# A decoder kernel's last feed-forward product turned to tokens by features, with the final norm done per token block

## The chip, the cores and the metric

The kernel runs on one core of a Trainium2 chip. The metric is the device time of one execution in microseconds; the kernel before takes 2560.55 us in the median of 3 runs (2559.9 to 2560.63). Everything is computed in float32 accuracy: each matrix product is made of three products of a high part and a low part (hi x hi, hi x lo, lo x hi), which TensorE takes in its fp32r form.

## What is computed

The reference is a decoder trunk for 1024 tokens of 1024 features: one recurrent layer, one attention layer, a SwiGLU feed-forward behind each, and a final RMSNorm. Cut to what the change touches (layer 1's feed-forward and the norm):

```python
def rmsnorm(x, g):
    y = x * lax.rsqrt(jnp.mean(x * x, axis=-1, keepdims=True) + EPS)
    return y * g

def swiglu(x, w_in, w_out):
    gate, up = jnp.split(x @ w_in, 2, axis=-1)
    return (jax.nn.silu(gate) * up) @ w_out

    # h: (1, 1024 tokens, 1024 features)
    h = h + mix
    h = h + swiglu(rmsnorm(h, norm_ffn[1]), w_ffn_in[1], w_ffn_out[1])   # D_FF = 2816
    return rmsnorm(h, norm_final)
```

## The kernel before

The residual `resid` lies in SBUF with features on the partitions: `resid[:, k, :]` holds features 128k to 128k+127 of all 1024 tokens. All products are made in that layout: weights are the stationary operand, 128 features by 128, and the tokens are the moving one, 512 at a time. A PSUM tile `ps[0]` to `ps[3]` is 128 x 1024 float32 (two banks), and a table of turns, `tiles`, says which of the four each step uses; `claim` (line 610) makes TensorE wait until the tile's last reader has counted up `drained`. Weight pieces go through four slots `raw`, `wh`, `wl` in the same way: SyncE loads them (`load`, line 427), ScalarE makes the high half (`split_hi`, line 963, its copy is line 974), VectorE the low half (`split_lo`, line 1316).

The feed-forward of layer 1 is `ffn(1)`, written for each engine. It runs over 11 groups of 256 hidden features. In each group from the second on, TensorE makes the gate tile G0, the eight output tiles of the group before (from `hh` and `hl`, the halves of the hidden values), the up tile U0, and then G1 and U1. An input tile (`in_tile`) is 48 matmuls of 128x512, an output tile 12. VectorE scales the gate (line 1353), ScalarE takes silu (1128), VectorE scales the up tile, multiplies (1581), ScalarE makes `hh` (1132), VectorE `hl` (1585); and VectorE adds each output tile to the residual (`add_tile`, line 1359). On ScalarE and VectorE the last group is written out behind the loop; on TensorE it is in the loop.

Behind the last group stands `out_epilogue` (line 693): the last group's own output tiles, 8 tiles of 12 matmuls. The first parts of three tiles, which need only the first half of the hidden values, are made ahead of the wait for the second half. Beside it the final norm is made ready. ScalarE squares each finished residual tile (line 994), GpSimd adds pairs of squares (line 578), and TensorE sums over features by 80 matmuls of one column against ones (`stat`, line 663), queued among the output tiles. VectorE multiplies the residual tiles by the final gain (`final_gain`, line 1547). Then a root (line 999) and a reciprocal (line 1346) give the factor of each token, TensorE transposes the residual, eight transposes of 128x128 for each of 8 token blocks (line 957), ScalarE and VectorE read one half of each block out of PSUM with the factor (lines 1304 and 1793), and SyncE stores it (line 510), 512 KB at a time, out of four buffers `tmp`.

The order on each engine is the order in which the program is written; there is no scheduler. The lines that matter for the turns are these:

```python
tiles.plan(f"ffn{f}A", [0, 1, 2, 3]).plan(f"ffn{f}L", [0, 1, 2, 3] * 3, GROUPS - 1, 1)
tiles.plan(f"ffn{f}E", OUT_STAT)        # OUT_STAT = [0, 1, 2, 0, 1, 2, 0, 1, 3]
tiles.plan("final", [0, 1, 2, 3] * 2)
```

Of the kernel before, what the change touches and what calls it, by code (L numbers as in the profile page):

```python
# [4 lines left out]
F32 = mybir.dt.float32  # L5
# [71 lines left out]
def hawk_fox_yoco(nc, x, norm_mix, norm_ffn, w_ffn_in, w_ffn_out, w_rec_in, conv_w, conv_b,  # L77
# [26 lines left out]
    V_MIX, V_FFN, V_KV, V_FINAL = 0, 2 * KT, 4 * KT, 5 * KT  # L104
    V_CONVB, V_LRU, V_CONVW, V_GATEB = 6 * KT, 7 * KT, 8 * KT, (8 + TAPS) * KT
# [27 lines left out]
    tiles.plan("final", [0, 1, 2, 3] * 2)  # L133
# [4 lines left out]
    STAT = {"start": 0, "recE": 1, "ffn0E": 2, "attE": 3, "ffn1E": 4}  # L138
# [6 lines left out]
    with ExitStack() as life:  # L145
# [9 lines left out]
        with ExitStack() as early:  # L155
            lru_alt = [sb(f"lru_alt{k}", [P, S], F32, early) for k in range(4)]
# [11 lines left out]
        row_rstd = sb("row_rstd", [P, QB], F32)  # L168
# [39 lines left out]
        hl = sb("hl", [P, 2, S], F32R)  # L208

# [81 lines left out]
        gained = sem("gained")  # L291
        rows_filled = sem("rows_filled")
        rows_ready = [sem(f"rows_ready{j}") for j in range(2)]
        rows_stored = [sem(f"rows_stored{b}") for b in range(4)]
# [37 lines left out]
        LRU_LAST = [tmp, lru_alt]  # L332
# [45 lines left out]
        def mean_of(seg):  # L378

            if seg == "ffn1E":  # L380
                return row_rstd[:, :], ps[3][:, 0:QB]
# [44 lines left out]
        def _(sp):  # L426
# [80 lines left out]
            for b in range(QB):  # L507
                for j in range(2):
                    sp.wait_ge(rows_ready[j], b + 1)
                sp.dma_start(out[0, b * P:(b + 1) * P, :], tmp[b % 4][:, :]).then_inc(rows_stored[b % 4], 16)  # L510
            for b in range(4):
                sp.wait_ge(rows_stored[b], 16 * (QB // 4))
# [3 lines left out]
        def _(pool):  # L516
# [86 lines left out]
            sum_squares("ffn1E")  # L603
# [3 lines left out]
        def _(pe):  # L607
# [43 lines left out]
            def stat(seg, n):  # L651
# [8 lines left out]
                if seg == "ffn1E":  # L660
# [1155 lines left out]
```

## Time and profile before

| what | value |
|---|---|
| median of 3 runs | 2560.55 us (2559.9 to 2560.63) |
| the profiled execution, its own time | 2558.25 us |
| its span, first to last instruction | 2556.4 us |
| TensorE matmul busy | 2446.8 us, 96% of the span |
| VectorE busy | 1271.8 us, 50% |
| ScalarE busy | 786.1 us, 31% |
| GpSimd busy | 124.8 us, 5% |
| mean granted TensorE clock | 0.98 of full |
| bytes moved | 122.63 MB, 48 GB/s on average |

In the page, PE is TensorE's matmuls, PEld its weight loads, DVE VectorE, ACT ScalarE, POOL GpSimd and SP SyncE. Times of rows are microseconds from the span's start. Where a row merges instructions, "x12" is how many; a matmul's duration is longer than the distance to the next one, since they are pipelined. A bracket at the end of a row is the idle time of the engine before it, and whom it waited for. A granted clock of 1.00 is 2.4 GHz, 0.50 is 1.2 GHz.

### The profile page before, as it was taken

What the parts mean: (1) busy time and instruction counts of PE and PEld (TensorE: products, weight loads), DVE (VectorE), ACT (ScalarE), POOL (GpSimd) and SP (SyncE); (2) the same over time, 40 slices, a digit from 0 to 9 for tenths busy, and PEclk for the clock granted to TensorE, in tenths of its full rate; (3) what the DMA queues carried; (4) which work ended last, traced back from release to release, by engine and by line L of the source; (5) the groups of instructions that cost most, each with busy time, mean ns of one, the idle gap of its engine ahead of it and who ended that gap; (6) DMA issues with size and microseconds to landing.
All of it is one profiled execution on the core that took longest, in us unless ns stands there. A gap on an engine that the chain in (4) does not pass through costs nothing.

```text
span 2556.4 us, 28698 instructions
## 1 busy us (share of the span) xinstructions
PE 2446.8 (96%) x11353; PEld 2009.7 (79%) x11353; DVE 1271.8 (50%) x1257; ACT 786.1 (31%) x1045; POOL 124.8 (5%) x80
## 2 busy tenths in 40 slices
PE   7999889999999999998999999979999999999998
PEld 5788768888888888867777777767788888888887
DVE  5767674434333434466665656553434444444344
ACT  4543542111111111145555555542211111111112
POOL 1000010000000000011110111001000000000001
PEclk9999999999999999999999999979999999999999
DMA  3111011111111111120111101021211111111111
GB/s 116 58 58 49 25 33 50 49 49 46 44 49 49 49 49 49 34 83 25 34 34 34 33 26 32 25 85 55 58 50 49 49 43 47 49 49 49 49 33 66
DMA packets 167166, 122.63 MB, mean 48 GB/s; under 512 B 5072, under 2 KB 148672, under 8 KB 167104
## 3 DMA queue, kind: packets, MB, share of 16 engines
q1 hardware_dynamic: 165360, 117.52, 15.1%
q10 hardware_dynamic: 1744, 4.32, 0.6%
q8 instruction: 35, 0.57, 0.1%
q14 instruction: 27, 0.22, 0.0%
HBM read 113.37 MB, written 8.45 MB: 48 GB/s over the span
## 4 chain that ended last, share of the span: by engine, by line
PE 88%; DVE 5%; ACT 3%; issue 3%; ACTq 1%; DMA 0%; POOL 0%; DVEq 0%
PE ps L619 66%; PE ps L804 8%; PE ps L915 3%; PE ps L851 3%; PE ps L838 2%; PE ps L819 1%; PE ps L667 1%; PE ps L816 1%; ACT kh L1190 1%; DVE rstd L1346 1%; DVE kv_tmp L1716 0%; PE ps L663 0%; DVE wl L1316 0%; DVE resid L1359 0%; ACT kh L1195 0%
## 5 line engine op out<-in xcount | busy, mean ns | idle before, releaser
L619 PE MATMUL ps<-xh,wh 128*128 128x512 f32 x1680 | 523.5, 393 | 10.6 <-DVE wl L1316 10.1
L619 PE MATMUL ps<-xl,wh 128*128 128x512 f32 x1680 | 518.2, 390 | 0.0
L619 PE MATMUL ps<-xh,wl 128*128 128x512 f32 x1680 | 518.0, 389 | 0.0
L619 PEld LDWEIGHTS ps<-xh,wh 128*128 128x128 f32 x1680 | 315.1, 188 | 81.4 <-issue 16.4
L1353 DVE TENSOR_TENSOR tmp<-ps,rstd 128x1024 f32<-128x1024 f32 x96 | 117.3, 1224 | 506.0 <-PE ps L619 506.0
L619 PEld LDWEIGHTS ps<-xh,wl 128*128 128x128 f32 x1680 | 315.7, 188 | 65.9
L619 PEld LDWEIGHTS ps<-xl,wh 128*128 128x128 f32 x1680 | 315.7, 188 | 65.7
L1359 DVE TENSOR_TENSOR resid<-ps,resid 128x1024 f32<-128x1024 f32 x216 | 261.6, 1222 | 187.9 <-PE ps L619 187.5
L974 ACT ACTIVATE wh<-raw 128x1024 fp32r<-128x1024 f32 x193 | 201.6, 1049 | 402.2 <-PE ps L619 349.7
L1316 DVE TENSOR_TENSOR wl<-raw,wh 128x1024 fp32r<-128x1024 f32 x193 | 238.8, 1241 | 169.6 <-ACT wh L974 169.5
L619 PE MATMUL ps<-hh,wh 128*128 128x512 f32 x704 | 219.4, 393 | 1.7 <-DVE hl L1585 1.7
L619 PE MATMUL ps<-hl,wh 128*128 128x512 f32 x704 | 217.8, 391 | 0.0
L619 PE MATMUL ps<-hh,wl 128*128 128x512 f32 x704 | 217.7, 390 | 0.0
L1132 ACT ACTIVATE hh<-tmp 128x1024 fp32r<-128x1024 f32 x44 | 46.7, 1061 | 480.1 <-DVE tmp L1581 480.1
L804 PE MATMUL ps<-xh,wh 128*128 128x512 f32 x384 | 160.1, 417 | 8.7 <-DVE wl L1316 5.5
L619 PEld LDWEIGHTS ps<-hh,wh 128*128 128x128 f32 x704 | 132.6, 189 | 31.2 <-DVE hl L1585 2.5
L619 PEld LDWEIGHTS ps<-hh,wl 128*128 128x128 f32 x704 | 132.8, 189 | 27.8
L619 PEld LDWEIGHTS ps<-hl,wh 128*128 128x128 f32 x704 | 132.7, 189 | 27.8
L804 PE MATMUL ps<-xh,wl 128*128 128x512 f32 x384 | 153.1, 399 | 0.0
L804 PE MATMUL ps<-xl,wh 128*128 128x512 f32 x384 | 153.0, 398 | 0.0
L1128 ACT ACTIVATE tmp<-tmp 128x1024 f32<-128x1024 f32 x44 | 46.6, 1059 | 322.9 <-DVE tmp L1353 322.9
L1734 DVE TENSOR_TENSOR ptl<-ps,pth 128x512 fp32r<-128x512 f32 (+1 forms) x160 | 98.3, 635 | 76.3 <-ACT pth L1253 74.8
(186 smaller groups left out, 2792.2 us busy)
## 6 DMA issues: line engine op xcount, KB each, us to landing
raw<-in_w_ffn_in SPq DMA_DIRECT2D x88, 512.0 KB, 3.8
raw<-in_w_ffn_out SPq DMA_DIRECT2D x44, 512.0 KB, 3.3
raw<-in_w_rec_in SPq DMA_DIRECT2D x16, 512.0 KB, 4.0
raw<-in_w_kvf SPq DMA_DIRECT2D x16, 512.0 KB, 3.9
xin<-in_x SPq DMA_DIRECT2D x4, 1024.0 KB, 10.1
raw<-in_w_rec_out SPq DMA_DIRECT2D x8, 512.0 KB, 4.0
raw<-in_w_q SPq DMA_DIRECT2D x8, 512.0 KB, 3.7
spill<-resid SPq DMA_DIRECT2D x8, 512.0 KB, 2.6
```

Source lines behind the costliest of these rows:

```text
L619: last = pe.matmul(acc[:, h], w, v[:, h], start=(first and p == 0), stop=(final and p == 2))
L804: last = pe.matmul(acc, w, v[:, k, h], start=(k == 0 and p == 0), stop=(k == KT - 1 and p == 2))
L838: last = pe.transpose(t_ps[t % 2][:, col + (q - q0) * P:col + (q - q0 + 1) * P], probs[u % 2][:, q, kb * P:(kb + 1) * P], ident[:, :])
L851: last = pe.matmul(o_ps[:, q0 * P:2 * P], v, pt[t % 2][:, col:col + n], start=(kb == 0 and pt is pth), stop=(kb == 2 * r + 1 and pt is ptl))
L915: last = pe.matmul(acc[:, h], w, ohl[:, k, v, h], start=(k == 0 and p == 0), stop=(k == KT - 1 and p == 2))
L974: act.activation(wh[slot][:, :], raw[slot][:, :], ACT.Copy).then_inc(hi_ready[slot], 1)
L1128: act.activation(tmp[t][:, :], tmp[t][:, :], ACT.Silu).then_inc(silu_ready, 1)
L1132: act.activation(hh[:, t, :], tmp[2 + t][:, :], ACT.Copy).then_inc(hh_ready, 1)
L1316: dve.tensor_tensor(wl[slot][:, :], raw[slot][:, :], wh[slot][:, :].bitcast(F32), ALU.subtract).then_inc(lo_ready[slot], 1)
L1353: dve.tensor_tensor(dst, ps[slot][:, :], rstd[:, :], ALU.mult).then_inc(drained[slot], 1)
L1359: dve.tensor_tensor(resid[:, m, :], ps[slot][:, :], resid[:, m, :], ALU.add).then_inc(drained[slot], 1)
L1734: dve.tensor_tensor(ptl[t % 2][:, 0:width], t_ps[t % 2][:, 0:width], pth[t % 2][:, 0:width].bitcast(F32), ALU.subtract).then_inc(ptl_ready, 1)
```

## The change

The last group's product is made the other way round. In `token_epilogue` a block of 128 tokens of `hh` or `hl` is the stationary operand, and the rows of the output weights (512 features at a time) are the moving one, so that a PSUM tile holds 128 tokens by 1024 features. That needs the residual in the same layout, and so it is transposed ahead: on TensorE the last group is written out behind the loop with tile turns of its own (`ffn1Z`), and `turn_block` puts four blocks of eight transposes behind its U0 tile and four behind its G1 tile. ScalarE copies each transposed block back over the same tokens of `resid` (`keep_rows`). In the tail, for each token block, VectorE adds the product to the residual rows (`add_rows`), ScalarE squares them with a sum over the row and takes the root, VectorE takes the reciprocal and multiplies by it and by the gain (`norm_rows`), and SyncE stores the block. The gain is a 128 x 1024 tile `gfinal`, loaded once by a broadcasting DMA ahead of the loop of `ffn(1)`; its 8 rows leave the vector tile `vec`, and one of the eight small loads on ScalarE's queue at the start goes with them. Gone are the squares by tile, GpSimd's three sums, the 80 one-column matmuls, the gain on resid, and the transposes and the two half reads at the end.

```diff
-        tiles.plan(f"ffn{f}A", [0, 1, 2, 3]).plan(f"ffn{f}L", [0, 1, 2, 3] * 3, GROUPS - 1, 1)
-        tiles.plan(f"ffn{f}E", OUT_STAT)
+        tiles.plan(f"ffn{f}A", [0, 1, 2, 3]).plan(f"ffn{f}L", [0, 1, 2, 3] * 3, GROUPS - 1 - f, 1)
+        if f == 1:
+            tiles.plan("ffn1Z", [0, 1, 2, 3] * 2 + [0, 1, 2, 3, 0, 2, 3, 0, 2, 1, 0, 2], 1, GROUPS - 1)
+        tiles.plan(f"ffn{f}E", OUT_STAT if f == 0 else [3, 1, 0, 2] * 2)
...
+        def token_rows(b):
+            return resid[:, :, b * P:(b + 1) * P]
+        def last_in(tile_seg, t):
+            return {9: 9, 10: 14, 11: 19}[t] if tile_seg == "ffn1Z" else t
+        def turn_tile(b):
+            return tiles.use("ffn1Z", 10 + b if b < 4 else 11 + b, GROUPS - 1)
+        def by_block(row):
+            return row.rearrange("p (k n) -> p k n", n=P)
...
+                if f == 1:
+                    sp.dma_start(gfinal[:, :], norm_final.rearrange("(a d) -> a d", a=1).broadcast_to([P, D])
+                                 ).then_inc(gfinal_loaded, 16)
                 with sp.Fori(1, GROUPS) as g:
...
-                for j in range(2):
-                    sp.wait_ge(rows_ready[j], b + 1)
-                sp.dma_start(out[0, b * P:(b + 1) * P, :], tmp[b % 4][:, :]).then_inc(rows_stored[b % 4], 16)
+                sp.wait_ge(final_ready, b + 1)
+                sp.dma_start(out[0, b * P:(b + 1) * P, :], rows_alt[b % 4][:, :]).then_inc(stored[b % 4], 16)
...
-            sum_squares("ffn1E")
...
-                if seg == "ffn1E":
-                    for b in range(QB):
-                        last = pe.matmul(ps[3][:, b:b + 1], sq(seg, k)[:, b * P:(b + 1) * P], ones[:, 0:1],
-                                         start=(n == 0 and b == 0), stop=(n == SUMS - 1 and b == QB - 1))
...
+                    for j in range(3):
+                        in_step(3 + j, last_in(tile_seg, 9 + j))
+                        for b in turns[j]:
+                            turn_block(b)
...
+                    with pe.Fori(1, GROUPS - 1) as g:
+                        body("ffn1L", g)
+                    body("ffn1Z", GROUPS - 1, (range(0, 4), range(4, 8), ()))
+                    token_epilogue()
+            def turn_block(b):
+                if b == 0:
+                    for m in range(4, 8):
+                        slot, n = tiles.use("ffn1Z", 1 + m, GROUPS - 1)
+                        pe.wait_ge(drained[slot], n)
+                acc = claim(turn_tile(b))
+                for k in range(KT):
+                    last = pe.transpose(acc[:, k * P:(k + 1) * P], resid[:, k, b * P:(b + 1) * P], ident[:, :])
+                last.then_inc(turned, 1)
+            def token_epilogue():
+                weights = [pieces.use("ffn1E", j) for j in range(2)]
+                def part(b, k):
+                    if k == 0:
+                        claim(tiles.use("ffn1E", b))
+                    acc, tok = ps[tiles.use("ffn1E", b)[0]], slice(b * P, (b + 1) * P)
+                    for v, terms in ((hh, (wh, wl)), (hl, (wh,))):
+                        for w in terms:
+                            for h, (slot, _) in zip(halves, weights):
+                                last = pe.matmul(acc[:, h], v[:, k, tok], w[slot][:, k * BANK:(k + 1) * BANK],
+                                                 start=(k == 0 and v is hh and w is wh), stop=(k == 1 and v is hl))
+                    if k == 1:
+                        last.then_inc(out_filled, 1)
+                for slot, n in weights:
+                    pe.wait_ge(lo_ready[slot], n)
+                pe.wait_ge(hl_ready, 4 * GROUPS - 1)
+                for b in range(3):
+                    part(b, 0)
+                pe.wait_ge(hl_ready, 4 * GROUPS)
+                for b in range(QB):
+                    if b >= 3:
+                        part(b, 0)
+                    part(b, 1)
...
+                def keep_rows(blocks):
+                    for b in blocks:
+                        slot, _ = turn_tile(b)
+                        act.wait_ge(turned, b + 1)
+                        act.activation(token_rows(b), by_block(ps[slot][:, :]), ACT.Copy).then_inc(drained[slot], 1)
...
                     h_high(grp, 0)
+                    if last and f == 1:
+                        keep_rows(range(0, 4))
                     if last:
                         split_hi(pieces.use(f"ffn{f}E", 0), FFN_END[f][0])
...
+                    if last and f == 1:
+                        keep_rows(range(4, 8))
+                    silu(tile_seg, last_in(tile_seg, 10), grp, 1)
...
             for b in range(QB):
+                slot, n = tiles.use("ffn1E", b)
+                act.wait_ge(drained[slot], n)
+                act.activation(by_block(tmp[b % 2][:, :]), token_rows(b), ACT.Square,
+                               accum_out=total[:, b:b + 1]).then_inc(total_ready, 1)
+                act.wait_ge(total_ready, b + 1)
+                act.activation(inv[:, b:b + 1], total[:, b:b + 1], ACT.Sqrt, scale=1.0 / D,
+                               bias=EPS).then_inc(token_root, 1)
...
+            def add_rows(b):
+                slot, _ = tiles.use("ffn1E", b)
+                dve.wait_ge(out_filled, OUT_FFN[1] + 8 * (GROUPS - 1) + b + 1)
+                dve.wait_ge(drained[turn_tile(b)[0]], turn_tile(b)[1])
+                dve.tensor_tensor(token_rows(b), by_block(ps[slot][:, :]), token_rows(b),
+                                  ALU.add).then_inc(drained[slot], 1)
+            def norm_rows(b):
+                dve.wait_ge(token_root, b + 1)
+                dve.reciprocal(inv[:, b:b + 1], inv[:, b:b + 1]).then_inc(inv_ready, 1)
+                dve.wait_ge(inv_ready, b + 1)
+                if b >= 4:
+                    dve.wait_ge(stored[b % 4], 16)
+                dve.scalar_tensor_tensor(out=by_block(rows_alt[b % 4][:, :]), in0=token_rows(b),
+                                         scalar=inv[:, b:b + 1], in1=by_block(gfinal[:, :]), op0=ALU.mult,
+                                         op1=ALU.mult).then_inc(final_ready, 1)
+            dve.wait_ge(gfinal_loaded, 16)
             for b in range(QB):
-                dve.wait_ge(rows_filled, b + 1)
-                if b >= 4:
-                    dve.wait_ge(rows_stored[b % 4], 16)
-                dve.tensor_scalar(tmp[b % 4][:, 0:BANK], ps[tiles.use("final", b)[0]][:, 0:BANK],
-                                  row_rstd[:, b:b + 1], None, ALU.mult).then_inc(rows_ready[0], 1)
+                add_rows(b)
+                if b >= 1:
+                    norm_rows(b - 1)
+            norm_rows(QB - 1)
```

## Rows read from the trace of the kernel before

**Rows 1.** Busy time by stretch: span, busy and count per engine, clock, DMA
```profile
1830.00:2504.90 674.90, 674.90 (x2979) 559.02 (x2978) 273.39 (x228) 107.59 (x106) 0.00 (x0) 1.00 0.16 47
2504.90:2556.40 51.50, 43.33 (x241) 38.10 (x239) 26.70 (x29) 16.54 (x19) 7.16 (x3) 0.89 0.21 82
```

**Rows 2.** Chain that ended last, in order of time: start, length, what
```profile
2379.97 125.13 PE ps L619 x552
...
2508.74 1.24 DVE hl L1585
...
2518.00 1.92 PE ps L663 x16
...
2534.39 6.79 PE ps L663 x48
```

**Rows 3.** Timeline, VectorE: the last half block that is read out
```profile
2550.89 0.75 DVE L1793 TENSOR_SCALAR tmp<-ps,row_rstd 128x512 f32<-128x512 f32 x1 [0.54 <-DMA out<-tmp]
```

**Rows 4.** Stores of line 510: from issue to landing
```profile
DMA to landing us min/median/max: 2.6/3.7/4.3
```

**Rows 5.** Timeline, ScalarE reading two transposed blocks in a row
```profile
2546.51 0.69 ACT L1304 ACTIVATE tmp<-ps,row_rstd 128x512 f32<-128x512 f32 x1 [0.19 <-PE ps L957]
2547.39 0.69 ACT L1304 ACTIVATE tmp<-ps,row_rstd 128x512 f32<-128x512 f32 x1 [0.19 <-PE ps L957]
```

**Rows 6.** Timeline, ScalarE's first split behind `hh` of the last group's U0
```profile
2486.85 1.05 ACT L974 ACTIVATE wh<-raw 128x1024 fp32r<-128x1024 f32 x1
```

**Rows 7.** Groups of instructions on ScalarE by form
```profile
L1253 ACT ACTIVATE pth<-ps 128x512 fp32r<-128x512 f32 x96 | 55.0, 597 | 87.3 <-PE ps L838 87.3
...
L994 ACT ACTIVATE tmp<-resid 128x1024 f32<-128x1024 f32 x32 | 33.5, 1047 | 19.5 <-DVE resid L1359 19.5
...
L1223 ACT ACTIVATION_READ_ACCUMULATOR probs<-ps,nmax 128x1 f32 x128 | 24.6, 192 | 0.0
...
L999 ACT ACT_TABLE_LOAD x4 | 5.1, 1283 | 0.1
```

**Rows 8.** Groups of instructions on VectorE by form
```profile
L1359 DVE TENSOR_TENSOR resid<-ps,resid 128x1024 f32<-128x1024 f32 x216 | 261.6, 1222 | 187.9 <-PE ps L619 187.5
...
L1393 DVE SCALAR_TENSOR_TENSOR tmp<-tmp,vec 128x1023 f32<-128x1023 f32 x8 | 10.3, 1284 | 0.3
...
L1701 DVE TENSOR_TENSOR ohl<-resid,ohl 128x1024 fp32r<-128x1024 f32 x8 | 11.4, 1485 | 0.0
...
L1346 DVE RECIPROCAL row_rstd<-row_rstd 128x8 f32<-128x8 f32 x1 | 0.2, 203 | 0.3 <-ACT row_rstd L999 0.3
```

**Rows 9.** Timeline, VectorE: adds in a row, and the first add of the tail
```profile
2455.17 2.35 DVE L1359 TENSOR_TENSOR resid<-ps,resid 128x1024 f32<-128x1024 f32 x2
...
2511.71 2.58 DVE L1359 TENSOR_TENSOR resid<-ps,resid 128x1024 f32<-128x1024 f32 x2 [1.75 <-PE ps L619]
```

**Rows 10.** Timeline, TensorE: first matmuls behind idle stretches of about 2 us
```profile
74.06 0.70 PE L619 MATMUL ps<-xh,wh 128*128 128x512 f32 x2 [2.23 <-DVE wl L1316]
...
345.91 0.78 PE L619 MATMUL ps<-yh,wh 128*128 128x512 f32 x2 [2.45 <-DVE yl L1428]
346.48 1.05 PE L619 MATMUL ps<-yl,wh 128*128 128x512 f32 x2
...
349.04 1.01 PE L619 MATMUL ps<-yl,wh 128*128 128x512 f32 x2
...
1677.50 1.80 PE L838 MATMUL ps<-ident,probs 128*128 128x128 f32 x8 [2.09 <-issue]
```

**Rows 11.** Windows, TensorE: span, busy and count, granted clock, DMA share, GB/s
```profile
2543.00:2544.00 1.00, 1.00 (x6) 0.50 0.00 0
2545.00:2546.00 1.00, 1.00 (x12) 1.00 0.97 397
```

**Rows 12.** Timeline: SyncE's loads ahead of the loop, ScalarE's use of one
```profile
1802.74 2.94 SPq L432 DMA_DIRECT2D raw<-in_w_ffn_in  x3
...
1837.63 1.05 ACT L974 ACTIVATE wh<-raw 128x1024 fp32r<-128x1024 f32 x1
```

More of the change, by code:

```diff
@@ L132, in hawk_fox_yoco @@
             tiles.plan("att", [1, 0, 1] + [0, 1] * (UNITS - 1) + [0], PAIRS).plan("attE", OUT_STAT)
-    tiles.plan("final", [0, 1, 2, 3] * 2)
     IN_FFN = [4 * BLOCKS, 4 * (BLOCKS + GROUPS)]
     OUT_FFN, OUT_ATT = [8 * BLOCKS, 8 * (BLOCKS + GROUPS + 1)], 8 * (BLOCKS + GROUPS)
-    STAT = {"start": 0, "recE": 1, "ffn0E": 2, "attE": 3, "ffn1E": 4}
+    STAT = {"start": 0, "recE": 1, "ffn0E": 2, "attE": 3}
     LRU_STEPS, FORGET_STEPS = 16, 10
@@ L155, in hawk_fox_yoco @@
         with ExitStack() as early:
-            lru_alt = [sb(f"lru_alt{k}", [P, S], F32, early) for k in range(4)]
+            rows_alt = [sb(f"rows_alt{k}", [P, S], F32, early) for k in range(4)]
         xl = sb("xl", [P, KT, S], F32R)
@@ L290, in hawk_fox_yoco @@
         ol_ready = sem("ol_ready")
[L291 to L294, printed above, removed]
+        gfinal_loaded = sem("gfinal_loaded")
+        turned = sem("turned")
+        token_rows_ready = sem("token_rows_ready")
+        total_ready = sem("total_ready")
+        token_root = sem("token_root")
+        inv_ready = sem("inv_ready")
+        final_ready = sem("final_ready")
+        stored = [sem(f"stored{b}") for b in range(4)]
         def cols(w, c0):
@@ L659, in stat @@
                     pe.wait_ge(sq_ready, STAT[seg] * KT + k + 1)
-                if seg == "ffn1E":
-                    for b in range(QB):
-                        last = pe.matmul(ps[3][:, b:b + 1], sq(seg, k)[:, b * P:(b + 1) * P], ones[:, 0:1],
-                                         start=(n == 0 and b == 0), stop=(n == SUMS - 1 and b == QB - 1))
-                else:
-                    for h in halves:
-                        last = pe.matmul(ps[3][:, h], ones[:, :], sq(seg, k)[:, h], start=(n == 0), stop=(n == SUMS - 1))
+                for h in halves:
+                    last = pe.matmul(ps[3][:, h], ones[:, :], sq(seg, k)[:, h], start=(n == 0), stop=(n == SUMS - 1))
                 last.then_inc(stat_filled if n == SUMS - 1 else sq_used, 1)
@@ new lines, in body @@
+                        for b in turns[j]:
+                            turn_block(b)
+                if f == 0:
+                    with pe.Fori(1, GROUPS) as g:
+                        body("ffn0L", g)
+                    out_epilogue("ffn0E", "ffn0E", hh, hl, hl_ready, 2 * GROUPS,
+                                 [(pieces.use("forget", 0), tiles.use("forget", 0), forget_filled)])
+                else:
+                    with pe.Fori(1, GROUPS - 1) as g:
+                        body("ffn1L", g)
+                    body("ffn1Z", GROUPS - 1, (range(0, 4), range(4, 8), ()))
+                    token_epilogue()
@@ L945, in _ @@
             ffn(1)
-            pe.wait_ge(gained, KT)
-            for b in range(QB):
-                if b < 4:
-                    acc = claim(tiles.use("final", b))
-                else:
-                    for j in range(2):
-                        pe.wait_ge(rows_ready[j], b - 3)
-                    acc = ps[b % 4]
-                for k in range(KT):
-                    last = pe.transpose(acc[:, k * P:(k + 1) * P], resid[:, k, b * P:(b + 1) * P], ident[:, :])
-                last.then_inc(rows_filled, 1)
         @block.scalar
@@ L1143, in body @@
                 def body(grp, last):
+                    tile_seg = "ffn1Z" if last and f == 1 else seg
                     split_hi(pieces.use(seg, 2, grp), ffn_free(f, 2, grp))
-                    silu(seg, 0, grp, 0)
+                    silu(tile_seg, 0, grp, 0)
                     split_hi(pieces.use(seg, 3, grp), ffn_free(f, 3, grp))
@@ L1543, in _ @@
             dve.memset(raw[slot][:, :], 0.0).then_inc(forget_dve, 1)
-            def final_gain(k):
-                dve.wait_ge(sq_ready, STAT["ffn1E"] * KT + k + 1)
-                dve.tensor_scalar(resid[:, k, :], resid[:, k, :], vec[:, V_FINAL + k:V_FINAL + k + 1], None,
-                                  ALU.mult).then_inc(gained, 1)
-            def behind(seg, k):
-                if seg == "ffn1E":
-                    final_gain(k)
-                else:
-                    low_half(seg, k)
             def epilogue(seg, out_count, nexts):
@@ L1599, in body @@
                 def body(grp, last):
+                    tile_seg = "ffn1Z" if last and f == 1 else seg
                     split_lo(pieces.use(seg, 2, grp))
-                    gate(seg, 0, grp, 0)
+                    gate(tile_seg, 0, grp, 0)
                     for j in range(2):
```

52 lines of the change are left out of this document (20 added, 32 removed).

## The prediction

> **What bounds the kernel now.** I read the busy shares by stretch first. In the feed-forward of layer 1 TensorE is busy the whole time, at full clock, with VectorE at 273 of 675 us and ScalarE at 108 [rows 1]: there a microsecond added to TensorE is a microsecond added to the end, and nothing else counts. The other stretch, from the end of the last group's U1 tile on, is different: 51.5 us in which TensorE is busy 43.3, at a clock of 0.89 [rows 1]. Only 96 of its matmuls are the product; the rest are one-column sums and transposes.
>
> The chain of waits says how the 51.5 us are spent. 552 matmuls of 128x512 take 125.13 us, 0.227 us each, and end at about 2505.1; the second half of the hidden values is ready at 2509.98 (2508.74 + 1.24) [rows 2]. The product needs 96 x 0.227 = 21.8 us. The sums over features take TensorE 1.92 us for the first sixteen and 6.79 for the last forty-eight [rows 2]. Then come 64 transposes, and only behind them the reads and the stores: the last half block is read out from 2550.89 to 2551.64 [rows 3], and the span ends 4.8 us later, at 2556.4. So this kernel does the whole normalisation and all eight stores behind the product. What is to be gained is that tail; what is to be paid is TensorE time ahead of it.
>
> I count from the moment the second hidden half is ready, T. Before, from T to the end are 2556.4 - 2510.0 = 46.4 us.
>
> **What the change adds ahead of T.** Sixty-four transposes. At full clock ScalarE's reads of two following blocks start 0.88 us apart, with ScalarE waiting for TensorE in between [rows 5], so a block of eight costs TensorE 0.88 us.
>
> First batch, behind U0. Time 0 is the end of U0. Blocks 0, 1, 2 go to tiles 2, 3, 0, which were drained long ago, and are done at 2.6. Block 3 goes to tile 2 again and must wait until ScalarE has copied block 0. ScalarE's queue has `hh` of U0 in front of that copy. In the trace U0 ends 21.8 us (96 matmuls of G1 and U1) ahead of 2505.0, at 2483.2, and ScalarE takes up its next instruction at 2486.85 [rows 6], 3.7 later. The 128x512 read of PSUM takes 0.60 us and the 1024-wide square 1.05 [rows 7], so a block of 1024 out of PSUM is about 1.05: block 0 is free at 4.75, block 1 at 5.75. TensorE stands idle from 2.6 to 4.8, does block 3 until 5.7, and G1, which goes to block 1's tile, starts at 5.8. Cost 5.8 us, of which 2.3 are idle. Queued behind the copies on ScalarE are the split of the next weights and, later, silu; the split is needed only at the tail. The bound below is 3.5 us (no idle time); above, if the scattered write into `resid` doubled the copy, 7.8.
>
> Second batch, behind G1. ScalarE is already waiting there. Blocks 4, 5, 6 find tiles 0, 2, 1 free; block 7 needs block 4's copy, done at about 2.2 where TensorE arrives at 2.6; U1 needs block 5's, done at 3.2 where TensorE arrives at 3.5. No idle time: 3.6 us with the change of operand. Silu of G1 is now behind four copies on ScalarE, at about 5.5, and is needed only when U1 is done, 14 us after G1. That waits for nobody.
>
> So T moves by 5.8 + 3.6 = 9.4 us, to 2519.4. The wait from U1's end to T stays as it is: the same four steps, with three first parts of TensorE's work beside them.
>
> **What happens behind T.** TensorE has the same 96 matmuls. 18 are done before T; 78 are left, 17.7 us at 0.227. Two parts of six are 2.72 us a block; blocks 0 to 2 come at 1.36 distance. The first is done at T + 1.36, and VectorE's add starts 1.7 behind T as now [rows 9]. Nothing else stands in TensorE's queue: the sums, the final transposes and the waits for GpSimd are gone.
>
> VectorE has per block an add, a reciprocal of one column and the product by factor and gain. Adds in a row follow each other at 1.13 us (2.35 for two, of which the last has its full 1.22) [rows 8, 9], the reciprocal on 8 columns takes 0.20 and the three-operand form 1.28 [rows 8]. With 0.05 of waiting between the last two that is 1.13 + 0.24 + 1.19 = 2.56 us a block, a little less than TensorE's 2.72, but the first blocks come faster than that and VectorE has a debt. ScalarE per block has a square of 1.05, the read of the accumulator 0.19 and a root of about 0.2 [rows 7]: 1.6 us with waits, never the bound, but for block 0 a table load of 1.28 for the root stands in it. Followed through: add 0 ends at 2.9, root 0 at 5.65 (with the load), norm 0 at 7.2, add 2 at 8.3, norm 1 at 9.8, and from there VectorE is never idle: add 7 ends at 21.2, norm 6 at 22.6. Square and root of block 7 are over by 22.7, its norm ends at T + 24.2. Had VectorE no debt it would be 22.3; with every three-operand product at the dearest row of its kind, 1.49 [rows 8], 25.8.
>
> The stores are spread 2.6 us apart, so the last goes alone: 0.1 to its issue, 2.6 to 3.7 to landing [rows 4], of which I take 2.8 since nothing is in its way, and 0.4 to the last instruction. End at T + 27.5.
>
> **Sum.** Before T: +9.4. Behind T: 27.5 in place of 46.4, -18.9. Together -9.5 us: span 2546.9. The profiled execution took 2558.25 us and the median is 2560.55; the difference, 2.3, is taken over, and the forecast is 2560.55 - 9.5 = 2551.0 us.
>
> Costed at nothing: the 512 KB load of the gain stands in SyncE's queue ahead of the loop's loads. The three loads around it are issued from 1802.74, and ScalarE uses the one that it pushes back at 1837.63 [rows 12]; landing takes a few us, so some 25 us cover it, and without them it would cost about 4. The small load that goes at the start saves between nothing and the time of one issue; the first matmul there waits for data while the large loads run, so I take nothing. Strided reads and writes of `resid` in runs of 128 values are in the trace at the same price as unbroken ones, as near as the 0.60 of the 512-wide copies goes [rows 7].
>
> **The clock, and a rule against the change.** After 2.23 us of idle time the clock stayed full, after 2.45 it fell: four pairs of matmuls at 1.05 to 1.01 us, from 346.48 to 349.9, 3.4 us for what 8 x 0.227 = 1.8 would do [rows 10]. Two us between groups of transposes (2.09) were followed by eight transposes at 1.80, half clock [rows 10]. The idle stretch of 2.2 us in my first batch lies in between. Where it falls, G1 starts at 1.2 GHz, and that costs 3.4 - 1.8 = 1.6 us; a stretch twice as long, as behind the forty-eight one-column matmuls, would cost 3.3.
>
> Transposes alone: at 2543 they ran at 0.50, and by 2545, with nothing but transposes on TensorE in between, the granted clock was 1.00 [rows 11]. So here they do hold or lift the clock. The Trainium skill (TensorE: Matmul & The Clock Gate, Part 4: PE-mode transpose) says the opposite, that a transpose doesn't count as TensorE activity in the same way and full clock doesn't engage for it; by it both batches would be quiet time, which is the third rival below. The trace speaks against it.
>
> **Rivals.**
> (1) The idle stretch in the first batch costs the clock: +1.6 us, 2552.7, up to 2554.4. For it the 2.09 row, against it the 2.23 row.
> (2) VectorE and the last store are dearer than I took: 25.8 behind T in place of 24.2, 3.7 for landing in place of 2.8, and ScalarE's copies into scattered `resid` 30% dearer (+0.6 in the first batch). +3.1, and with the clock of rival 1, 2555.8. That is no measurable change.
> (3) Transposes count as idle time: both batches (5.8 and 3.6 us) are quiet, half clock in part of them and behind each, 1.6 and 2.7 us: 2555.3. Against it [rows 11].
> (4) The change loses: ScalarE's tables. The tail alternates Square and Sqrt. If each pair costs two loads of 1.283 us [rows 7], a block takes ScalarE 1.05 + 0.19 + 0.2 + 2.57 + waits = 4.07 us, more than TensorE's 2.72, and ScalarE sets the tail: root 7 at T + 2.9 + 2.8 + 7 x 4.07 = 34.2, its norm at 35.8, the end at T + 39.1, which is 2558.5 for the span, +2.1: 2562.6 us. It decides from a ScalarE block time of about 3.8 us on. Against it: five roots run at line 999 with only four loads, and none of the 32 squares at line 994 has one, though some of them follow a root and a root follows them [rows 7]. So Square runs under the root's tables.
>
> **How the numbers follow.** Forecast 0.45; rival 1 0.27; rival 2 0.14; rival 3 0.07; rival 4 0.07. The bounds of the forecast itself are 3.5 for the first batch in place of 5.8 and 22.3 in place of 24.2 behind T, -4.2 together, which I don't expect to meet at once; half of that gives 2548.9. Upward the range goes to rivals 1 to 3, 2555.8. A measurement of this kernel tells about 0.2% from no change, 5.1 us; faster means under 2555.4. The forecast, rival 1 and half of rivals 2 and 3 lie there: 0.82. Same: 0.12, the rest of 2 and 3 and some of 4. Slower by over 0.2%: 0.06.
>
> **What the profile after would show.** Right: G1 of the last group starts about 5.8 us after U0's last matmul with an idle stretch of 2.2 us ahead of block 3; U1 3.6 after G1; the span ends 27 to 28 us behind the last `hl`; VectorE without a gap from the third block on; one table load in the tail; stores that don't overlap. Wrong: a clock of 0.50 inside G1 (rival 1) or in both tiles (rival 3), VectorE durations over 1.3 us in the tail (rival 2), sixteen table loads there (rival 4), or an idle TensorE at part 4 or later because a tile's add is late.

## The result, and the profile of the changed kernel

| | before | after |
|---|---|---|
| median of 20 runs each (lowest to highest) | 2559.76 us (2557.95 to 2562.09) | 2564.2 us (2562.22 to 2567.99) |
| ratio of the times, 95% interval | | 1.0018, 1.0011 to 1.0025 |
| span of the profiled execution | 2556.4 us | 2561.7 us |

The changed kernel is slower, by 0.18%. The forecast was 2551.0 us with a range that ended at 2555.8. So the sign was wrong, and 13 us have to be found. The page of the changed kernel opens with its span and its busy times: TensorE is busy for 2448.5 us with 11273 matmuls, and it was 2446.8 us with 11353 before. That is more time for fewer instructions:

```profile
span 2561.7 us, 28516 instructions
PE 2448.5 (96%) x11273; PEld 1996.8 (78%) x11273; DVE 1268.3 (50%) x1255; ACT 790.1 (31%) x1060; POOL 117.7 (5%) x77
```

**The end of the program, step by step.** The busy times by stretch (span, busy and count per engine, clock, DMA) answer to [rows 1]. They are cut where those were, 21.8 us behind the end of U0; there the kernel before had both remaining tiles done, while here the batches of transposes have come in between. Behind the cut are 41.6 us, in place of 51.5.

```profile
1845.00:2520.10 675.10, 673.01 (x2982) 554.35 (x2981) 269.69 (x225) 111.18 (x111) 0.00 (x0) 1.00 0.15 47
2520.10:2561.70 41.60, 32.15 (x139) 25.63 (x137) 25.18 (x28) 14.91 (x28) 0.00 (x0) 0.94 0.25 101
```

The timeline of the two batches of transposes (start, length, engine, line, operation, idle time before it and what ended it):

```profile
2498.33 2.78 PE L830 MATMUL ps<-ident,resid 128*128 128x128 f32 x24
...
2501.04 1.06 ACT L1185 ACTIVATE hh<-tmp 128x1024 fp32r<-128x1024 f32 x1 [12.32 <-DVE tmp L1632]
2502.12 3.77 ACT L1191 ACTIVATE resid<-ps 128x1024 f32<-128x1024 f32 x4
...
2503.20 1.09 PE L830 MATMUL ps<-ident,resid 128*128 128x128 f32 x8 [2.09 <-ACT resid L1191]
...
2504.11 0.74 PE L639 MATMUL ps<-xh,wh 128*128 128x512 f32 x2
...
2515.22 3.65 PE L830 MATMUL ps<-ident,resid 128*128 128x128 f32 x32
2518.63 0.70 PE L639 MATMUL ps<-xh,wh 128*128 128x512 f32 x2
```

First batch: 2504.11 - 2498.33 = 5.78 us, with 2.09 idle, ended by ScalarE's copy of block 0. Second batch: 2518.63 - 2515.22 = 3.41 us, nothing idle. Behind them the tail:

```profile
2533.43 1.22 DVE L1636 TENSOR_TENSOR hl<-tmp,hh 128x1024 fp32r<-128x1024 f32 x1 [1.13 <-ACT hh L1185]
...
2536.47 2.57 DVE L1843 TENSOR_TENSOR resid<-ps,resid 128x1024 f32<-128x1024 f32 x2 [1.82 <-PE ps L844]
...
2538.90 1.28 ACT L1366 ACT_TABLE_LOAD   x1
...
2540.43 0.16 DVE L1848 RECIPROCAL inv<-inv 128x1 f32<-128x1 f32 x1 [1.39 <-ACT inv L1366]
...
2540.62 1.29 DVE L1852 SCALAR_TENSOR_TENSOR rows_alt<-resid,inv,gfinal 128x1024 f32<-128x1024 f32 x1
...
2541.94 17.03 SPq L531 DMA_DIRECT2D out<-rows_alt  x8
...
2557.32 1.29 DVE L1852 SCALAR_TENSOR_TENSOR rows_alt<-resid,inv,gfinal 128x1024 f32<-128x1024 f32 x1
```

T, the moment the second hidden half is ready, is 2534.66 here (2533.43 + 1.22, to rounding). VectorE's last product by factor and gain ends at 2558.61, which is T + 23.95, and the span ends at T + 27.0. VectorE waits 1.39 us once, for the first root behind its table load, and never again. From the end of U0 to the end of the span are 63.4 us. Before there were 73.2, from the first matmul of G1 to 2556.4:

```profile
2483.17 0.61 PE L619 MATMUL ps<-xh,wh 128*128 128x512 f32 x2
```

The edited part of the program gained 9.8 us; 9.5 were forecast.

**So the loss is ahead of it.** U0 of the last group ends at 2498.33 in place of 2483.2, 15.1 us later, in code that the change doesn't edit. The chain of waits doesn't show a new wait: TensorE is unbroken from the start of layer 1's feed-forward to the end of the last group's U0. In the chain of work that ended last (start, length, what, count):

```profile
1829.95 668.55 PE ps L639 x2928
```

What is longer is every group. VectorE's first read behind the output tiles of each group is a clock that ticks once a group. Of the kernel before:

```profile
2222.25 1.23 DVE L1353 TENSOR_TENSOR tmp<-ps,rstd 128x1024 f32<-128x1024 f32 x1 [8.52 <-PE ps L619]
2233.13 1.23 DVE L1353 TENSOR_TENSOR tmp<-ps,rstd 128x1024 f32<-128x1024 f32 x1 [4.82 <-PE ps L619]
...
2287.53 1.23 DVE L1353 TENSOR_TENSOR tmp<-ps,rstd 128x1024 f32<-128x1024 f32 x1 [8.52 <-PE ps L619]
```

and of the changed kernel:

```profile
2235.48 1.22 DVE L1415 TENSOR_TENSOR tmp<-ps,rstd 128x1024 f32<-128x1024 f32 x1 [8.56 <-PE ps L639]
2246.47 1.22 DVE L1415 TENSOR_TENSOR tmp<-ps,rstd 128x1024 f32<-128x1024 f32 x1 [4.93 <-PE ps L639]
2257.35 1.23 DVE L1415 TENSOR_TENSOR tmp<-ps,rstd 128x1024 f32<-128x1024 f32 x1 [6.36 <-PE ps L639]
...
2301.24 1.23 DVE L1415 TENSOR_TENSOR tmp<-ps,rstd 128x1024 f32<-128x1024 f32 x1 [8.56 <-PE ps L639]
```

A group takes 65.76 us in place of 65.28. The tile G1 takes 10.99 in place of 10.88, U1 still 10.88. Most of the rest lies in the eight output tiles of a group: TensorE's timeline has them 22.09 us long in place of 21.76, and U0 behind them 10.92 in place of 10.88. Twenty groups at 0.48 are 9.6 us.

By VectorE's clock and TensorE's timeline in the two profiled executions, the 15.1 us are 4.9 in the feed-forward of layer 0, 4.8 in that of layer 1 up to U0's end, 4.9 in attention and 0.5 in all that stands before layer 0's feed-forward. The two feed-forward figures repeat from execution to execution. The other two don't: with the experiments below there are six profiled executions in which the tiles' distances are those of the kernel before or differ from them by 256 bytes, and between layer 0's last clock tick and layer 1's first they take 751.7 us in two (the kernel before and the later run e4) and 754.5 to 754.7 in four. The changed kernel takes 756.6. So of the 4.9 us of attention some 2.9 can be such a difference between executions, and the changed kernel surely adds only 2.1. What makes this difference isn't shown. The granted clock has its half stretches at other places in the one kind of execution than in the other. These are TensorE's busy time, granted clock, DMA share and GB/s from 1225 to 1245 us, in the kernel before and in the changed kernel with its tiles back in place (e2 below):

```profile
1225.00:1245.00 20.00, 17.78 (x87) 1.00 0.18 53
```

```profile
1225.00:1245.00 20.00, 17.60 (x79) 0.91 0.19 53
```

But that stretch alone doesn't decide: in e5, below, which moves none of attention's tiles, there is one at 1236 us, and attention takes 752.2 us.

Within the output tiles there are two paces. Starts of pairs of matmuls in the changed kernel, first inside the second half of the output tiles (weights O1), then inside U0 that follows:

```profile
2480.86 0.63 PE L639 MATMUL ps<-hl,wh 128*128 128x512 f32 x2
2481.33 0.63 PE L639 MATMUL ps<-hh,wl 128*128 128x512 f32 x2
2481.80 0.63 PE L639 MATMUL ps<-hh,wh 128*128 128x512 f32 x2
...
2490.61 0.62 PE L639 MATMUL ps<-xl,wh 128*128 128x512 f32 x2
2491.07 0.61 PE L639 MATMUL ps<-xh,wl 128*128 128x512 f32 x2
2491.52 0.62 PE L639 MATMUL ps<-xh,wh 128*128 128x512 f32 x2
```

The first lie 0.467 us apart, at a granted clock of 1.00. U0 (but for its first five pairs, at 0.462 in the mean) and the first half of the output tiles (weights O0, but for its first two pairs) have 0.453, as all of them had before. G1 has 0.458. The same instruction, with the same shape, at the same clock, costs 3% more for one set of weights.

**What differs is where the tiles lie.** Tiles are laid out in SBUF in the order of their allocation. The change takes 8 columns out of `vec` and drops `row_rstd`, 32 bytes a partition each. So everything allocated behind both lies 64 bytes lower: `raw`, `wh`, `wl` of slots 2 and 3, `tmp`, `hh`, `hl`, the attention tiles. `resid`, `xh`, `xl` and the weights of slots 0 and 1 stay. The byte addresses in a partition, worked out from the allocations in the two kernels:

| | `xh` | `wh0` | `wh2` | `hh` | `wh0` to `hh` |
|---|---|---|---|---|---|
| before | 49280 | 127104 | 153984 | 186752 | 59648 = 233 x 256 |
| after | 49280 | 127104 | 153920 | 186688 | 59584 = 232.75 x 256 |

The pieces of a group use the weight slots G0 1, O0 2, O1 0, U0 1, G1 2, U1 0. In the changed kernel the pair is made of one moved and one unmoved tile in O1 (`hh` with slot 0) and in G1 (`xh` with slot 2), and these two are slow. In O0 both are moved, in G0, U0 and U1 neither, and these are fast. Before the change all these distances are multiples of 256 bytes.

### The profile page after: what moved, and what is told of

Same layout as the page of the kernel before. It is cut to its first block, busy times and chain, and to the rows that moved or that the text cites. A ratio compares the mean times of both kernels' runs of the same rounds, so it can differ in the third digit from the quotient of the medians.

```text
span 2561.7 us, 28516 instructions
## 1 busy us (share of the span) xinstructions
PE 2448.5 (96%) x11273; PEld 1996.8 (78%) x11273; DVE 1268.3 (50%) x1255; ACT 790.1 (31%) x1060; POOL 117.7 (5%) x77
## 3 DMA queue, kind: packets, MB, share of 16 engines
q1 hardware_dynamic: 165504, 118.04, 15.1%
## 4 chain that ended last, share of the span: by engine, by line
PE 87%; DVE 5%; issue 3%; ACT 3%; ACTq 0%; POOL 0%; DMA 0%; DVEq 0%
PE ps L639 66%; PE ps L871 8%; PE ps L982 3%; PE ps L918 3%; PE ps L905 2%; PE ps L886 1%; PE ps L681 1%; PE ps L883 1%; ACT kh L1254 1%; DVE rstd L1408 1%; DVE kv_tmp L1768 0%; DVE wl L1378 0%; DVE kl L1709 0%; ACT kh L1259 0%; PE ps L948 0%
## 5 line engine op out<-in xcount | busy, mean ns | idle before, releaser
L1421 DVE TENSOR_TENSOR resid<-ps,resid 128x1024 f32<-128x1024 f32 x208 | 251.8, 1222 | 185.5 <-PE ps L639 185.5
L1378 DVE TENSOR_TENSOR wl<-raw,wh 128x1024 fp32r<-128x1024 f32 x193 | 237.9, 1236 | 179.0 <-ACT wh L1028 178.8
L639 PE MATMUL ps<-hh,wh 128*128 128x512 f32 x672 | 211.0, 395 | 0.7 <-DVE hl L1636 0.7
L639 PE MATMUL ps<-hl,wh 128*128 128x512 f32 x672 | 209.3, 393 | 0.0
L639 PE MATMUL ps<-hh,wl 128*128 128x512 f32 x672 | 209.1, 392 | 0.0
L639 PEld LDWEIGHTS ps<-hh,wh 128*128 128x128 f32 x672 | 126.5, 188 | 30.5 <-issue 1.5
L639 PEld LDWEIGHTS ps<-hl,wh 128*128 128x128 f32 x672 | 126.5, 188 | 28.6
L639 PEld LDWEIGHTS ps<-hh,wl 128*128 128x128 f32 x672 | 126.2, 188 | 28.4
```

The costliest lines, as they stand in the source:

```text
L639: last = pe.matmul(acc[:, h], w, v[:, h], start=(first and p == 0), stop=(final and p == 2))
L1378: dve.tensor_tensor(wl[slot][:, :], raw[slot][:, :], wh[slot][:, :].bitcast(F32), ALU.subtract).then_inc(lo_ready[slot], 1)
L1421: dve.tensor_tensor(resid[:, m, :], ps[slot][:, :], resid[:, m, :], ALU.add).then_inc(drained[slot], 1)
```

## The experiments

Theory A: the pace of these matmuls depends on the placement of the operands relative to each other, and the 64 bytes are the whole loss. Theory B: the new code itself disturbs the loop (another program, other tile turns). None of the kernels leaves out any of the computation. Each kernel was timed beside the kernel before, and its ratio is to those runs; their medians are 2560.29 us (for e1 to e4), 2559.8 (e5 to e8) and 2559.96 (e9 and e10). In the tables "group" is the distance between two ticks of VectorE's clock as shown above.

**e1: the kernel before, with the 64 bytes, and nothing else.**

```diff
         row_rstd = sb("row_rstd", [P, QB], F32)
+        sb("pad", [P, 16], F32)
```

> The kernel before with one unused tile of 64 bytes a partition behind row_rstd, so that everything allocated later (the second pair of weight slots, tmp, hh, hl, the attention tiles) starts 64 bytes past a multiple of 128, as it does in the changed kernel, while resid, xh, xl and weight slots 0 and 1 stay on a multiple of 128. Not one instruction differs. Theory L (the 15 us that the changed kernel loses ahead of its last group come from where the tiles lie): about +16 us over before, matmul pairs of the second four output tiles of a group at 0.467 us in place of 0.453, a group of the feed-forward at 65.76 us in place of 65.28. Rival C (they come from the new code: the loop of TensorE one turn shorter, the last group written out, the extra load of the gain): no change, within 1 us.

Measured: 2572.01 us, ratio 1.0045 (1.0031 to 1.0059), span 2570.5. Its VectorE timeline:

```profile
2234.31 1.22 DVE L1354 TENSOR_TENSOR tmp<-ps,rstd 128x1024 f32<-128x1024 f32 x1 [8.53 <-PE ps L620]
2245.51 1.23 DVE L1354 TENSOR_TENSOR tmp<-ps,rstd 128x1024 f32<-128x1024 f32 x1 [5.13 <-PE ps L620]
...
2300.10 1.22 DVE L1354 TENSOR_TENSOR tmp<-ps,rstd 128x1024 f32<-128x1024 f32 x1 [8.54 <-PE ps L620]
```

A group takes 65.79, G1 takes 11.20. An unused tile makes the kernel before 11.7 us slower; about 16 were expected. The shift goes the other way here (+64), and so do the two paces: G1 has the slow one, and O1, expected at 0.467 us a pair, has 0.458 (10.99 us for its 48 matmuls).

**e2: the changed kernel, with its tiles back in place.**

```diff
         lru = sb("lru", [P, 6, KT], F32)
+        sb("pad", [P, 16], F32)
```

> The changed kernel with one unused tile of 64 bytes a partition behind lru, so that the later tiles lie again where they lay before. Theory L: the 15 to 16 us come back and the saving of the tail shows, span about 2546.5, 9 to 11 us under before, ratio 0.996. Rival C: still 4 to 5 us slower than before.

Measured: 2549.05 us, ratio to before 0.9957 (0.9944 to 0.9971), span 2547.2. The group is 65.28 again (2222.99 to 2288.27), the end of U0 is at 2483.91, and the batches cost what they did:

```profile
2488.79 1.09 PE L831 MATMUL ps<-ident,resid 128*128 128x128 f32 x8 [2.09 <-ACT resid L1192]
...
2500.71 3.65 PE L831 MATMUL ps<-ident,resid 128*128 128x128 f32 x32
```

One unused tile takes 14.5 us off the span. Theory B falls: the new code is all there, and the loss isn't. What is left of the 15.1 is 0.7 us between this U0 and that of before, and that is a difference between executions: this one is 2.1 us ahead at layer 0's first clock tick and takes 2.8 us longer in attention. In the tail, where `hh` is the stationary operand and the weights are the moving one, the mean pair goes from 0.462 us back to 0.453 too. By stage this run is ahead of the changed kernel by 2.6 us before layer 0's feed-forward, 4.9 in it, 2.1 in attention and 4.8 in layer 1's. The medians agree: 0.9957 against 1.0018 of the kernel before is 15.6 us.

**e3: all tiles moved together.** Is it the absolute address?

```diff
+        sb("pad", [P, 16], F32)
         resid = sb("resid", [P, KT, S], F32)
```

> The kernel before with the unused 64 bytes ahead of resid, the first tile: all tiles move by 64 bytes together. If what counts is how the two operands of a matmul lie to each other (theory L relative), no change, within 1 us. If it is the distance of each one from a multiple of 128 (theory L absolute), slower than e1, over +20 us. Rival C: no change.

Measured: 2560.94 us, ratio 1.0002 (0.9993 to 1.0011), group 65.28 (2224.54 to 2289.82). The absolute address doesn't matter, the distances do.

**e5: only the hidden values moved.** Which distance?

```diff
+        sb("pad", [P, 16], F32)
         hh = sb("hh", [P, 2, S], F32R)
```

> The kernel before with the unused 64 bytes directly ahead of hh, so that only hh and hl move by 64 bytes and all weight slots and xh, xl stay. Theory L in its relative form: the output tiles of both weight slots are slow now, since both slots lie 64 bytes off hh; the input tiles, G1 among them, are at full pace; a group's output tiles take 22.1 to 22.4 us in place of 21.76, a group 65.6 to 65.9, the kernel +7 to +13 us. If the weights' place alone counted: no change.

Measured: 2564.41 us, ratio 1.0021 (1.0012 to 1.0030), span 2561.2, group 65.56. VectorE's clock shows that G1 is fast again:

```profile
2226.19 1.22 DVE L1354 TENSOR_TENSOR tmp<-ps,rstd 128x1024 f32<-128x1024 f32 x1 [8.57 <-PE ps L620]
2237.07 1.22 DVE L1354 TENSOR_TENSOR tmp<-ps,rstd 128x1024 f32<-128x1024 f32 x1 [4.82 <-PE ps L620]
...
2291.75 1.23 DVE L1354 TENSOR_TENSOR tmp<-ps,rstd 128x1024 f32<-128x1024 f32 x1 [8.57 <-PE ps L620]
```

Both halves of the output tiles, whose weights have not moved while `hh` and `hl` have, go at 0.458 us a pair; the input tiles at 0.453, but for the first pairs of U0. So it is the moving operand against the stationary one. The loss, 4.6 us in the medians, is under the 7 to 13 that I had expected, and the group just under its 65.6: both slow pieces take 10.99 to 11.00 us here, while in e1 one of the two slow pieces takes 11.20.

**e6, e7, e9 and e10: how coarse is the grain?** The same place as the first experiment, with other widths:

```diff
         row_rstd = sb("row_rstd", [P, QB], F32)
+        sb("pad", [P, 8], F32)
```

> e1 with 32 bytes in place of 64. Theory L with any offset: as slow as e1, +10 to +16 us. Theory L with 64 bytes as the grain that counts: no change, within 2 us.

```diff
         row_rstd = sb("row_rstd", [P, QB], F32)
+        sb("pad", [P, 32], F32)
```

> e1 with 128 bytes in place of 64: the later tiles start on a multiple of 128 again. Theory L: no change, within 1.5 us. If any moved tile or any added tile costs time: +10 us or more.

```diff
         row_rstd = sb("row_rstd", [P, QB], F32)
+        sb("pad", [P, 48], F32)
```

> The kernel before with 192 unused bytes behind row_rstd. The later tiles then lie to the earlier ones as in the changed kernel, if 256 bytes is the period: the distance from weight slot 0 to hh is 59648 bytes before, a multiple of 256, and 59584 in the changed kernel. The 128 of e7 was not harmless, so the grain is larger than theory L first had it. Theory L with a period of 256: the changed kernel's pace to the hundredth, 65.76 us a group, slow O1 and G1, and the U0 tile of the last group ending at about 2498 in place of 2483.2; span about 2571.5. Theory that any moved tile costs time by its amount: between e7 and more, +17 to +25.

```diff
         row_rstd = sb("row_rstd", [P, QB], F32)
+        sb("pad", [P, 64], F32)
```

> The same with 256 bytes. Period 256: no change, within 1.5 us, 65.28 us a group. Period 512 or more, or any moved tile costs: slow, +10 us or more.

| shift of the later tiles, bytes | median, us | ratio to before (95%) | span | group |
|---|---|---|---|---|
| 0 (before) | 2559.76 | | 2556.4 | 65.28 |
| 32 | 2578.34 | 1.0074 (1.0060 to 1.0087) | 2576.2 | 65.99 |
| 64 | 2572.01 | 1.0045 (1.0031 to 1.0059) | 2570.5 | 65.79 |
| 128 | 2576.55 | 1.0069 (1.0055 to 1.0083) | 2574.7 | 65.90 |
| 192 | 2575.15 | 1.0060 (1.0046 to 1.0073) | 2572.4 | 65.76 |
| 256 | 2560.46 | 1.0000 (0.9991 to 1.0009) | 2558.9 | 65.28 |

The expectation that 128 bytes would do no harm was wrong: the grain is coarser. And 32 bytes cost 18.5 us, more than the 10 to 16 expected. The period was then tested with 192, which is -64 but for a whole 256, and with 256. Their timelines:

```profile
2236.06 1.23 DVE L1354 TENSOR_TENSOR tmp<-ps,rstd 128x1024 f32<-128x1024 f32 x1 [8.56 <-PE ps L620]
2247.05 1.23 DVE L1354 TENSOR_TENSOR tmp<-ps,rstd 128x1024 f32<-128x1024 f32 x1 [4.93 <-PE ps L620]
...
2301.82 1.22 DVE L1354 TENSOR_TENSOR tmp<-ps,rstd 128x1024 f32<-128x1024 f32 x1 [8.56 <-PE ps L620]
```

```profile
2225.04 1.23 DVE L1354 TENSOR_TENSOR tmp<-ps,rstd 128x1024 f32<-128x1024 f32 x1 [8.52 <-PE ps L620]
2235.92 1.23 DVE L1354 TENSOR_TENSOR tmp<-ps,rstd 128x1024 f32<-128x1024 f32 x1 [4.82 <-PE ps L620]
...
2290.32 1.23 DVE L1354 TENSOR_TENSOR tmp<-ps,rstd 128x1024 f32<-128x1024 f32 x1 [8.52 <-PE ps L620]
```

With 192 bytes the kernel before has the very signature of the changed one: group 65.76, G1 10.99, the output tiles 22.09 with 0.467 a pair in O1. With 256 it is the kernel before again. So the pace follows the distance modulo 256 bytes, as far as these six points go, and the changed kernel's distance explains its loop to the hundredth.

Put by distance (moving operand less stationary one, modulo 256), the pieces of all these kernels fall into line. The times are TensorE's for the 48 matmuls of one piece:

| distance | pieces | us |
|---|---|---|
| 0 | all in the kernel before, e2, e3, e4, e8, e10 | 10.88 |
| 64 | G1 of the changed kernel and of e9; O1 of e1; O0 and O1 of e5 | 10.99 to 11.00 |
| 192 | O1 of the changed kernel and of e9; G1 of e1 | 11.20 |
| 32 and 224 | O1 and G1 of e6 | 11.20 and 11.19 |
| 128 | O1 and G1 of e7 | 11.15 and 11.16 |

A piece at distance 0 right behind a slow one takes up to 10.94. A shift of 64 and one of 192 only swap the two pieces, and so their groups are nearly the same, 65.79 and 65.76.

**e4: better batches.** The first batch stood idle for 2.09 us because its fourth block goes to a tile that isn't drained. With three blocks behind U0 and five behind G1 nothing is waited for. On top of the changed kernel with its pad:

```diff
-            tiles.plan("ffn1Z", [0, 1, 2, 3] * 2 + [0, 1, 2, 3, 0, 2, 3, 0, 2, 1, 0, 2], 1, GROUPS - 1)
-        tiles.plan(f"ffn{f}E", OUT_STAT if f == 0 else [3, 1, 0, 2] * 2)
+            tiles.plan("ffn1Z", [0, 1, 2, 3] * 2 + [0, 1, 2, 3, 0, 1, 2, 3, 0, 2, 3, 1], 1, GROUPS - 1)
+        tiles.plan(f"ffn{f}E", OUT_STAT if f == 0 else [2, 0, 3, 1] * 2)
...
-                        keep_rows(range(0, 4))
+                        keep_rows(range(0, 3))
...
-                        keep_rows(range(4, 8))
+                        keep_rows(range(3, 8))
```

(and the same split where the turns and the loop's ranges name it.)

> e2 with the eight transposed blocks placed as three behind U0 and five behind G1, G1 going to the tile that U0 leaves and U1 to the one that G1 leaves, so that TensorE waits for no copy of ScalarE in the first batch. The idle stretch of 2.1 us goes and so does the wait of G1: 2.1 to 2.3 us less than e2 if TensorE's time is the path there, as forecast; the same as e2 if something else ends last.

Measured: 2548.66 us, ratio to before 0.9955 (0.9942 to 0.9969), span 2544.0. TensorE's timeline has 24 transposes from 2483.09 and the next matmul at 2485.63, then 40 from 2496.62 and the next at 2500.91: 2.54 + 4.29 = 6.83 us for both batches, where the changed kernel has 5.78 + 3.41 = 9.19. The 2.4 us show in the span (3.2 less, of which 0.8 lie ahead of the batches); in the medians, 2549.05 and 2548.66, they can't be told from the scatter.

**e8: the root's table loaded early.** A root of one column, ahead of the tail, on top of the last kernel:

```diff
+            act.activation(warm[:, :], ones[:, 0:1], ACT.Sqrt)
             for b in range(QB):
                 slot, n = tiles.use("ffn1E", b)
```

> e4 with one root of one column on ScalarE ahead of the tail, so that the table for roots is loaded before block 0 is squared. If VectorE's debt sets the end, as the forecast had it (VectorE stands 1.4 us before its first reciprocal and never again), the norm of block 0 and all that follows come about 1.3 us earlier, span about 2542.7. If TensorE's last part sets the end, nothing changes.

(The tile `warm` is allocated last and moves no other.) Measured: 2545.74 us (2542.17 to 2547.63), ratio to before 0.9945 (0.9931 to 0.9958), span 2544.1. The load now lies beside VectorE's `hl`, and VectorE's first reciprocal doesn't wait:

```profile
2517.08 1.28 ACT L1362 ACT_TABLE_LOAD   x1
2517.09 1.23 DVE L1639 TENSOR_TENSOR hl<-tmp,hh 128x1024 fp32r<-128x1024 f32 x1 [1.13 <-ACT hh L1187]
...
2522.80 0.16 DVE L1851 RECIPROCAL inv<-inv 128x1 f32<-128x1 f32 x1
```

From T to the end of VectorE's last product are 22.66 us in place of 23.93 in the kernel without it: 1.3 gained. The span doesn't show it, because U0 of this execution ended 1.4 us later, at 2484.47: it is one of the four that take 754.5 us in attention, and the kernel without it, e4, one of the two that take 751.7. This kernel is faster than the kernel before by 0.55% and the fastest that was run; its interval overlaps those of the two other changed kernels that keep the distances.

## Why the prediction was wrong

By its own steps:

- **First batch**: forecast 5.8 us with about 2.3 idle; 5.78 with 2.09. The copy's length, 1.05 taken from [rows 7], was 0.94 (3.77 for four). Held.
- **Second batch**: forecast 3.6, measured 3.41. Held.
- **Behind T**: first add forecast at T + 1.7, measured at T + 1.8; a block 2.56 against 2.52, norm 7 at T + 24.2 against T + 23.95; end T + 27.5 against T + 27.0. The reciprocal cost 0.16 where [rows 8] had 0.20, the product by factor and gain 1.29 as the 1.28 row said, not 1.49. The claim that strided access to `resid` costs no more cites rows that show a copy without strides; it held all the same, with 1.22 us for an add on token rows.
- **The sum of the edited part**: -9.5 forecast, -9.8 measured.
- **Costed at nothing, held**: the gain's load in SyncE's queue delayed nobody, since TensorE is unbroken from 1829.95 on. The small load gone at the start can't be seen: the first matmul on weights starts at 23.62 in place of 24.31, but in the eight profiled executions that still have that load it starts between 23.41 and 24.32.
- **The step that failed** is in the sum: "Together -9.5 us: span 2546.9" presumes that everything ahead of the last group takes what it took. I had counted instructions, queues and waits, and apart from the gain's load and the small load at the start the change touches none of them there. It does touch the allocation list: 8 columns of `vec` and `row_rstd`. I read both lines of the diff and gave them no cost and no bound, not even as an unknown. They cost 14.4 us of the 15.1 by which the last group came late, by the run with the pad (its U0 ends at 2483.91, not at 2498.33), give or take the 2 us by which executions differ ahead of layer 0's feed-forward. Its span of 2547.2 is 0.3 above the forecast of 2546.9, and its median, 2549.05, lies in the range from 2548.9 to 2555.8. That the span agrees so closely is partly luck: the 2.1 us by which this execution was ahead and the 2.8 by which its attention was longer nearly cancel.

**The rivals.** Rival 1 (the clock falls in the first batch's idle stretch) fell. These are the granted clocks through both batches, from TensorE's busy time by windows (start and end, length, busy time and count, granted clock, DMA share, GB/s). The windows are the end of the first three blocks with the start of the idle time, the rest of the idle time, the fourth block, G1 behind it, then the second batch and U1 behind it:

```profile
2500.40:2502.40 2.00, 0.71 (x7) 1.00 0.00 0
2502.40:2503.20 0.80, 0.00 (x0) 1.00 0.00 0
2503.20:2504.10 0.90, 0.90 (x8) 1.00 0.00 0
2504.10:2505.10 1.00, 1.00 (x6) 1.00 0.00 0
2505.10:2507.10 2.00, 2.00 (x10) 1.00 0.00 0
2515.40:2517.40 2.00, 2.00 (x20) 1.00 0.00 0
2518.60:2520.60 2.00, 2.00 (x12) 1.00 0.00 0
```

It is 1.00, the 2.4 GHz level, everywhere. An idle stretch of 2.09 us left it there, in this kernel and in the one with the pad; in [rows 10] a stretch of 2.09 stood ahead of transposes at half clock. So the length of the stretch alone doesn't decide. What does isn't settled here.

Rival 2 (VectorE and the last store dearer) fell: no product by factor and gain took over 1.29 us, and the end came at T + 27.0.

Rival 3 (transposes count as idle time) fell with the same rows: a granted clock of 1.00 inside the transposes of both batches and behind them. The Trainium skill (TensorE: Matmul & The Clock Gate, Part 4: PE-mode transpose) says that full clock doesn't engage for a transpose. By that rule the transposes would not have helped to hold the clock; the trace disagrees, with 1.00 through 3.65 us of transposes in a row and behind them.

Rival 4 (ScalarE's tables) fell: one table load in the tail, at 2538.90, for eight squares and eight roots. Yet the kernel did end slower, at 2564.2 where this rival had 2562.6. That is chance: its mechanism was absent, since ScalarE was never the bound.

**What stays open.** Which access inside the chip collides when the distance is off; why the first five pairs of U0, whose tiles have not moved, are slow as well; why a distance of 64 costs a third of what 192 costs; how much of attention's 4.9 us and of the difference ahead of layer 0's feed-forward is placement and how much differs from execution to execution; and which matmuls there lose it, since tiles of many kinds moved at once and were not moved one by one. The run with the pad gives back 2.1 us in attention. The feed-forwards' 9.7 us are the part that was taken apart piece by piece.

## What to carry to other kernels

A tile that is resized, dropped or added moves every tile allocated behind it, so a diff's allocations belong in the sum like its instructions. Where TensorE sets the time, compare the byte addresses of moving and stationary operands before and after, keep their distances as they were, or whole multiples of 256 bytes from them (an unused tile does it), and if a kernel changes pace in code that nobody touched, look there first. The time of one loop iteration in a stage that the change leaves alone, read in both traces, finds such a loss quickly. And where two traces are compared stage by stage, a second execution of the same program tells how much of a stage's difference is none: here attention alone varied by 2.9 us.

## What the runs showed of the hardware

- The pace of the 128x512 matmuls depends on the distance in SBUF between the moving and the stationary operand: 0.453 us a pair where it was a multiple of 256 bytes (0, 256 and all tiles moved together), 0.458 to 0.467 where it was not, at the same granted clock of 1.00. The sign counts: moving less stationary 64 bytes cost 0.458, 192 bytes 0.467. In the kernel before the four shifts of 32 to 192 bytes cost 11.7 to 18.5 us of 2560, by their medians.
- The idle stretch of 2.09 us between transposes left the clock at 1.00, and so did 3.65 us of transposes in a row.
- Alternating squares and roots on ScalarE took one table load of 1.28 us in all.
